# Experts of a hybrid diffusion step: the next block's tokens are transposed inside the gate and up product

## The reference, cut to what matters

```python
gates = jnp.einsum('nk,nke->ne', g_w * top_w, jax.nn.one_hot(expert_id, N_EXPERTS, dtype=jnp.float32))
hid = jax.nn.silu(jnp.einsum('nd,edf->nef', x, w1)) * jnp.einsum('nd,edf->nef', x, w3)
out = jnp.einsum('nef,efd->nd', hid * gates[:, :, None].astype(hid.dtype), w2)
```

## Time and profile before

| what | us |
|---|---|
| median of 3 runs | 2050.86 (2044.34 to 2053.27) |
| profiled execution, its own time | 2052.82 |
| its span | 2051.0 |
| PE busy | 1825.6 (89%) |
| DVE busy | 1050.7 (51%) |
| ACT busy | 800.6 (39%) |

### The profile page before, as it was taken

The page is one execution under the profiler, slowest core; times in us unless marked ns, Lnnn a source line. Parts: engine busy times, 40 slices in busy tenths (PEclk is TensorE's granted clock), DMA queues, the critical chain, the costliest instruction groups (busy, mean ns, idle before and its releaser), DMA issues. The chain is left out here.

```text
span 2051.0 us, 28828 instructions
## 1 busy us (share of the span) xinstructions
PE 1825.6 (89%) x11512; PEld 1528.7 (75%) x11512; DVE 1050.7 (51%) x1597; ACT 800.6 (39%) x1085; POOL 248.8 (12%) x242
## 2 busy tenths in 40 slices
PE   6899898999999998799939998989999999939992
PEld 2898555679999984588729975556799999727781
DVE  3322566762323456788772226477522334558884
ACT  3320251662212231678662103516521223217883
POOL 0102410000000000244310043100000000003430
PEclk8899999999999998899959999999999999969996
DMA  9213301311222426899772223021211225148984
GB/s 363 78 41 86 137 1 63 106 60 63 83 62 70 158 102 247 336 366 361 283 263 74 74 45 137 25 100 63 63 62 62 84 81 195 64 169 335 371 328 187
DMA packets 128104, 299.92 MB, mean 146 GB/s; under 512 B 10808, under 2 KB 53496, under 8 KB 119288
## 3 DMA queue, kind: packets, MB, share of 16 engines
q1 hardware_dynamic: 110808, 264.15, 35.8%
q0 software_dynamic: 9792, 20.99, 2.7%
q10 hardware_dynamic: 7392, 13.19, 2.3%
HBM read 283.25 MB, written 29.72 MB: 153 GB/s over the span
## 5 line engine op out<-in xcount | busy, mean ns | idle before, releaser
L1920 PE MATMUL pair<-hT_r,mid_r 128*128 128x320 f32 x768 | 237.3, 309 | 0.0
L1920 PE MATMUL pair<-r_r,ring_r 128*128 128x320 f32 x832 | 211.8, 309 | 2.2 <-DVE ring_r L1278 2.2
L1920 PE MATMUL pair<-mid_r,r_r 128*128 128x512 f32 (+1 forms) x528 | 193.1, 366 | 19.5 <-DVE hT_r L1710 19.5
L1920 PE MATMUL pair<-ysT_r,mid_r 128*128 128x256 f32 (+1 forms) x768 | 171.9, 315 | 12.5 <-DVE r_r L1234 12.5
L2001 PE MATMUL pair<-cst,mid 128*128 128x128 f32 x748 | 122.1, 305 | 66.3 <-DVE mid L1224 31.0
L1920 PE MATMUL pair<-mid_r 128*128 128x320 f32 x576 | 178.9, 311 | 1.6 <-issue 1.6
L1920 PE MATMUL pair<-r_r,mid_r 128*128 128x256 f32 (+2 forms) x576 | 180.0, 313 | 0.0
L2001 PEld LDWEIGHTS pair<-cst,mid 128*128 128x128 f32 x748 | 94.5, 155 | 114.4 <-DVE mid L1224 38.9
L1920 PE MATMUL pair<-mid_r,ring_r 128*128 128x320 f32 x576 | 178.0, 309 | 0.0
L1507 DVE TENSOR_TENSOR r<-pair,r 128x640 f32<-128x640 f32 x48 | 39.5, 823 | 252.3 <-PE pair L1920 252.3
L1920 PEld LDWEIGHTS pair<-r_r,ring_r 128*128 128x128 f32 x832 | 145.8, 188 | 2.7 <-DVE ring_r L1278 2.7
(11 more groups left out here) (284 smaller groups left out, 4007.7 us busy)
## 6 DMA issues: line engine op xcount, KB each, us to landing
ring<-in_w_mod SPq DMA_DIRECT2D x23, 2048.0 KB, 8.3
ring<-in_w_gate SPq DMA_DIRECT2D x34, 1024.0 KB, 8.2
ring<-in_w_up SPq DMA_DIRECT2D x34, 1024.0 KB, 10.1
ring<-in_w_down SPq DMA_DIRECT2D x34, 1024.0 KB, 8.3
ring<-in_w_in SPq DMA_DIRECT2D x24, 1024.0 KB, 6.9
ring<-in_w_in SPq DMA_DIRECT2D x8, 2048.0 KB, 10.9
ring<-in_w_branch SPq DMA_DIRECT2D x12, 1024.0 KB, 5.1
ring<-in_w_out SPq DMA_DIRECT2D x8, 1024.0 KB, 5.1
```

Source lines behind the costliest of these rows:

```text
L1920: return nc.tensor.matmul(out, lhsT, rhs, start=first, stop=last, skip_group_check=True)
```

## The change

Three orders change. PE: the eight transposes of the next block's tokens stand between the fourth and the fifth of the eight slices of `up`. ScalarE: `round_tokens` stands ahead of `gate_values`. VectorE: `remainder_tokens` stands ahead of `hidden`.

```diff
--- before
+++ after
@@ -1129,9 +1129,9 @@
 
                 def block_rounds(b, s, rnd, first, last):
 
-                    gate_values(b, s)
                     if not (last and s):
                         round_tokens(b + 1, 1 - s)
+                    gate_values(b, s)
                     round_down(s, rnd)
                     round_hidden(b, s)
                     if not (first and s == 0):
@@ -1729,9 +1729,9 @@
 
                 def block_remainders(b, s, last):
 
-                    hidden(b, s)
                     if not (last and s):
                         remainder_tokens(1 - s, b * 5 + 6)
+                    hidden(b, s)
                     remainder_down(s, b * 5 + (4 if last and s else 7))
                     remainder_hidden(s, b * 5 + (5 if last and s else 8))
                     if not last:
@@ -2298,7 +2298,7 @@
                         last = nc.tensor.transpose(pair[0][:, k * P:(k + 1) * P], xg[:, s, k * P:(k + 1) * P], ident)
                     last.then_inc(t_filled, 1)
 
-                def up(b, s):
+                def up(b, s, more):
 
                     pe.wait_ge(t_freed, b + 2)
                     pe.wait_ge(down_ready, b + 1)
@@ -2307,6 +2307,8 @@
                     high = w13_high[s].rearrange("p (j k f) -> p k j f", j=2, k=KD)
                     out = pair[1][:, s * 512:(s + 1) * 512]
                     for k in range(KD):
+                        if k == KD // 2 and more is not None:
+                            gathered(b + 1, 1 - s, more)
                         x, x_rest = [x[:, k * P:(k + 1) * P] for x in xg_parts[s]]
                         mm(out, x, high[:, k], k == 0, False)
                         mm(out[:, 0:FF], x, gate_low[s][:, k * FF:(k + 1) * FF], False, False)
@@ -2335,9 +2337,7 @@
 
                 def block(b, s, rnd, first, last):
 
-                    up(b, s)
-                    if not (last and s):
-                        gathered(b + 1, 1 - s, rnd + s)
+                    up(b, s, None if last and s else rnd + s)
                     if not (first and s == 0):
                         down(b - 1, 1 - s)
                     turn_hidden(b, s)
```

## The result

The changed kernel takes 2055.65 us (median of 18 runs, 2052.12 to 2062.18) against 2050.88 us (18 runs, 2044.12 to 2056.3) before: a ratio of 1.0026, with a 95% interval of 1.0015 to 1.0037. The time is within 0.5% of that of before, as forecast, but the interval lies wholly above 1. The change costs 4.8 us where the forecast had 1.4. The profiled execution took 2053.89 us, with a span of 2052.1.

A forecast was written before the change was run, and what follows sets the result against it. The stream of DMA transfers was taken as the stage's bound. Terms of +0.4 us (0.2 once in each layer) and +1.0 us at the heads gave +1.4 on the median of 2050.86, written as 2052 us, range 2041 to 2064.

The forecast's parts named there:

- What bounds the stage: Stage of the experts: the stream of transfers is the bound; 3.3 to 4.2 us of a gate load's time is queueing.
- The later issue of the gate load is absorbed: Steady blocks: gate load issued 1.2 us later, within its queueing; nothing per block, 0.2 us once in each layer.
- The wait moves from line 1710 to line 1715: TensorE's wait moves from `up` (token remainder) to `turn_hidden` (`hidden`), 0.5 to 1 us each.
- The mis-sized term: GpSimd's gather, released by `t_filled`, goes out 2.8 us earlier and moves the same rows; no cost was given.
- The hole at the head, +0.8 and +0.2 us: Stage start, DMA engines empty: `h_filled` 1.03 us later widens the gap, +0.8 us in one layer, +0.2 in the other.
- +1.0 us for the heads: Total charged for the start of the stage over both layers, between −1.7 and +2.0 us.
- no change within 0.5%: Whole kernel: time within 10 us of before, chance 0.76.
- The head's gain of 0.85 us: First block of the stage: with early tokens the second `up` follows `turn_hidden` at once, 0.85 us gained.
- Latency as the bound: Rival: fixed 8 to 9 us from gate load issue to landing; 0.6 us a block slower, +16 us, 2067; chance 0.13.
- The wait that simply goes: Rival: TensorE's waits for the token remainder come from queue order alone and vanish; 14.7 us gained, 2036; chance 0.11.
- The clock: TensorE's granted clock may fall to 0.50 in one or two more places or one less: −1.7 to +3.4 us.
- the forecast case: Whole kernel: the summed terms with their spreads, clock included, around 2052; with run spread 2046 to 2060 us.

The follow-up runs named there:

- gather_held: The full change, with GpSimd's gather also waiting for the end of the running `up`, so it goes out behind the gate load: 2050.16 us.
- after_early: The full change, with the eight `up` products that read the gate's slot made first and releasing the gate load, gather not held: 2046.55 us.
- before_early: The kernel before, with the eight `up` products that read the gate's slot made first and releasing the gate load: 2049.41 us.
- held_loop: The full change, with the gather held until the end of `up` only in the loop, from the fifth block on: 2052.25 us.
- queues_only: The kernel before with only the ScalarE and VectorE orders changed, the transposes left behind `up`: 2059.28 us (7 runs).

## Why the prediction was right, and which term was mis-sized

**What bounds the stage: right.** Halving one of three loads shortened the block by 0.39 us (0.28 without the slow place of the clock; 0.55 was expected) and took away nearly all of the gate waits; releasing the gate load earlier in the kernel before did nothing. Both say stream, not latency.

**The later issue of the gate load is absorbed: right in the steady stretch.** The medians to landing fell from 8.1 and 8.6 to 6.9 and 6.5 us, somewhat more than the 1.2 us forecast, ScalarE's waits for it kept their size, though not their number (7 for 12 in layer 1), and the period stayed between 10.0 and 10.4 us, at 10.19 and 10.24.

**The wait moves from line 1710 to line 1715: right.** 4.6 us in 8 waits and 4.9 in 7, a mean of 0.6 and 0.7 us, at `turn_hidden`.

**The mis-sized term** is the sentence "GpSimd's gather, released by `t_filled`, goes out earlier by the same 2.8 us; it moves the same rows". It was costed at nothing. The rows are the same, but the order among the transfers is not: 2.8 us earlier is ahead of the gate load instead of 1.9 us behind it, and the gate load is the one that somebody waits for. At the head, where I had charged +1.0 us for a later `h_filled`, the two heads lost 2.7 us (0.7 and 2.0), since the gate load needed 6.0 and 7.6 us instead of 4.9 and 4.8. Per block, where I had nothing, 1.3 and 1.6 us were lost over the layers (3.0 in layer 0 without the slow place of the clock in the trace of before). With the 0.3 us that the last blocks give back, that is 5.3 us by the trace and 4.8 by the medians; with the gather behind the gate load again, it is gone as far as can be measured (`gather_held`). The numbers were all there and were never set side by side: the gather 1.9 us behind the gate load, minus 2.8 us for the earlier transposes and 1.0 us for the later gate load, is 1.9 us ahead of it; 1.8 was measured.

**The hole at the head, +0.8 and +0.2 us: not borne out.** With the gather held, the gate load still goes out later by the transposes, and ScalarE waits for it (0.78 us), but TensorE only 0.29, and the head of layer 1 is 19.26 us, shorter than the 19.72 of before. The kernel before had 0.7 us to spare at this place, as its ScalarE row at 1859.61 shows. So the +1.0 us for the heads stood for a cost that wasn't there, and hid part of one that was.

**How much the number says.** The forecast of no change within 0.5% was right, but its range of 2041 to 2064 would have held a cost more than twice as large. That the miss in the gather's term stayed inside it is owed to the size of that term and not to the reasoning, which left it out; in that much it was luck.

**The head's gain of 0.85 us: right.** It was lost behind the late gate weights in the full change and shows in `after_early`, whose heads are 0.8 us shorter than before.

**The rivals.** Latency as the bound would have given +16 us, and `before_early` a gain; neither came. The wait that simply goes would have given −14.7 us; the chain behind the landing held both orders, as argued. The clock played a small part, as the forecast case allowed: the one slow place of the kernel before (1.7 us) is missing in the trace of the changed one, whose steady windows stand at 1.00, and its heads had the low clock a little longer (0.6 us). What the clock was worth in the executions that were not profiled is not known.

**What stays open.** How the loss in the steady stretch comes about block by block was not resolved: that it belongs to the gather's place is shown by `held_loop` and `gather_held` only as a sum. Why a gather of 0.36 MB delays the load behind it by 2.8 us, when its packets account for 0.6 to 0.9, is not shown. And 5.5 of the 8.4 us of `queues_only` are not explained.

## What to carry to other kernels

When a change moves a signal, list every transfer that the signal releases, on every queue, and write their new order on the shared DMA engines next to the old one: a transfer that nobody waits for can cost time by getting ahead of one that somebody does. If an early signal is wanted for its data, hold the transfer back with a second wait, or release the urgent load earlier still, as `after_early` does; that turned a loss of 4.8 us into a gain of 4.6 against the kernel before. And if a result comes out within the noise of the forecast but with an interval on one side, it is worth a few runs: the term costed at nothing was worth 5.5 us (`gather_held`).

## What the runs showed of the hardware

- An indirect gather of up to 128 rows (138 packets, 0.36 MB), issued 1.8 us ahead of a 1 MB load from another engine, stretched that load from 4.8 to 7.6 us in one layer and from 4.9 to 6.0 in the other. In the first 2.5 us behind its issue the load moved 0.14 MB where it had moved 0.39 without the gather.
- A 1 MB load that found the DMA engines empty moved 157 GB/s over the first 2.5 us behind its issue and 410 GB/s from 2.3 to 3.8 us behind it. It landed 4.8 to 4.9 us after its issue in three places (1854.10 and 843.73 before, 1854.40 in `gather_held`, there by ScalarE's start).
- TensorE reached a busy share of 98% (107.99 of 110 us) at a DMA share of 0.92. At 0.97, with all the bytes, it had 96%, and ScalarE waited for weights.
- From the first `up` of a layer, behind waits of TensorE for tokens of 9.8 and 12.9 us in the kernel before, the granted clock stood at 0.50 for a time that differs from execution to execution: the mean over the first six us was 0.76 and 0.76 before, 0.68 and 0.74 after, 0.51 in layer 0 of `gather_held`. The last is 1.0 us of work less than the 0.68.
